# Cache compression as a ring of token-pair steps, with three split float32r products

## The chip, the core and the metric

The kernel runs on one core of a Trainium2 chip. The metric is device time in microseconds, the median of the runs. The core has five engines that run their own instruction lists and wait for each other by semaphores: TensorE (PE; its weight loads are shown as PEld), VectorE (DVE), ScalarE (ACT), GpSimd (POOL) and SyncE (SP). ACT, POOL and SP also issue DMAs.

## What is computed

One inference step of a decoder layer for a prompt of 1024 tokens and for 8 sequences that each have 8192 cached tokens and add one. The change is in the compression of the cache of the 8 sequences:

```python
r = CMP_BLOCK // CMP_STRIDE                      # 32 / 16 = 2
pieces = kv[:, :(n_c + r - 1) * CMP_STRIDE].reshape(b, n_c + r - 1, CMP_STRIDE, NSA_KV_HEADS, HEAD_DIM)
hid = sum(jnp.einsum('bncgd,cdf->bngf', pieces[:, p:p + n_c] + pe_r[p][:, None, :], w1_r[p]) for p in range(r))
return jnp.einsum('bngf,fd->bngd', jax.nn.gelu(hid), w2)
```

It is done for keys and for values (kv = 0, 1), for 8 sequences and 2 heads g of 64 channels. A sequence has 512 pieces of 16 tokens; a block is two pieces next to each other, so there are 511 blocks. The hidden width is 256. The cache lies in pages of 128 tokens, which a page table names. Beside it, the adaLN modulation is computed, c @ w_ada + b_ada, for 9 rows and 64 groups of 128 columns. All of it is float32.

## The kernel before

The kernel is a chain of stages with a barrier after each (`stage_done`); inside a stage the engines' lists are written by hand, each with its own semaphore waits.

The first stage, `setup`, loads the page table, turns two small tables, spreads the relative bias over 8193 distances on DVE (32 copies into `rev`), stores that table to HBM, and starts the loads of the compression weights, of the first modulation weights and of the first pages. Its store of 2 MB ends it.

The second, `cache_compress`, has 16 items, (i, kv), for 8 sequences i. An item's 64 pages go into `raw[:, kv]`, 32 by SP and 32 by POOL (`load_page`, line 168), once PE has turned what lay there. PE turns the pages, 16 tokens s of each piece, four 128 x 128 transposes each, into four banks (line 346). DVE copies the even tokens and ACT the odd ones into `xt` (line 412), so that a matmul contracts over two tokens of 64 channels. The first product (`first`, line 354) takes, for each of four quarters n = (g, c), a head and a half of the 256 hidden columns, 16 matmuls over 511 columns in fp32, each of which is two instructions in the profile. ACT applies the gelu (line 457), PE the second product (`second`, lines 366 and 369), DVE copies the result (line 423) and ACT stores it (lines 469 and 471). A quarter also has one of four pieces of the modulation (line 380, 16 instructions of 9 columns) and a quarter of the transposes of the item that follows. The position bias `peb` is a set of 128 one-column instructions ahead of it all (line 331).

Behind it come `load_x` (line 505 is its first DMA) and further stages. `mlstm_project` (line 649) is the third one after; its DVE list begins with two memsets and then waits for projections of the values (line 755). The last stages, merge, output and feed-forward, already use three split products: a float32 operand is rounded to float32r (ACT, line 2261), the rest is its difference (DVE, line 2285), and `mm3` (line 1909) sums high x high, high x low and low x high.

Of the kernel before, what the change touches and what calls it, by code (L numbers as in the profile page):

```python
# [34 lines left out]
B = 8  # L35
# [127 lines left out]
def load_page(k, eng, i, page, kv):  # L163
# [4 lines left out]
    eng.dma_start(k.raw[8 * q:8 * q + 8, kv, nt], pages[bass.ds(at, 1), :, :, P * kv:P * kv + P]  # L168
                  .rearrange("o n s c -> (o n) s c")).then_inc(k.s_page[kv][nt], 16)


def setup(k):

    nc = k.nc
    s_const, s_rows, s_vec, s_cT, s_cTs = (k.sem(x) for x in ("s_const", "s_rows", "s_vec", "s_cT", "s_cTs"))
    s_tab, s_rev, s_neg, s_fwd, s_store = k.sem("s_tab"), k.sem("s_rev"), k.sem("s_neg"), k.sem("s_fwd"), k.sem("s_bstore")
    with ExitStack() as ctx:
        crow = k.sb("crow", [9, D], ctx=ctx)  # L180
        vrow = k.sb("vrow", [NVEC, P], ctx=ctx)
        tab = k.sb("tab", [64, NBUCKET], ctx=ctx)
        rev = k.sb("rev", [64, NREV], ctx=ctx)
        fwd = k.sb("fwd", [H, NFWD], ctx=ctx)
        block = ctx.enter_context(nc.Block())
        ends = BUCKET_START[1:] + [PAST + 1]

        @block.sync
        def _(sp):
            sp.dma_start(k.pt[:, :], k.i["page_table"].rearrange("b n -> (b n)").rearrange("(o n) -> o n", o=1)).then_inc(k.s_pt, 16)  # L190
            sp.dma_start(crow[0:1, :], k.i["c_prompt"]).then_inc(s_rows, 16)
            sp.dma_start(crow[1:9, :], k.i["c_sample"]).then_inc(s_rows, 16)
            for name, (r, n) in VEC.items():
                a = k.i[name]
                a = a[0] if len(a.shape) == 2 else a
                sp.dma_start(vrow[r:r + n, :], a.rearrange("(r p) -> r p", p=P)).then_inc(s_vec, 16)
            sp.wait_ge(k.s_pt, 16)
            load_pages(k, sp, 0, 0, 0)

        @block.gpsimd  # L200
        def _(pool):
            pool.memset(k.ident[:, :], 0.0).then_inc(s_const, 1)
            pool.memset(k.ones[:, :], 1.0).then_inc(s_const, 1)
            pool.wait_ge(s_const, 2)
            pool.affine_select(out=k.ident[:, :], in_=k.ident[:, :], compare_op=ALU.not_equal, fill=1.0,
                               base=0, pattern=[[-1, P]], channel_multiplier=1).then_inc(s_const, 1)
            pool.wait_ge(k.s_pt, 16)
            load_pages(k, pool, 0, 0, 1)

        @block.tensor  # L210
        def _(pe):
            pe.wait_ge(s_const, 3)
            pe.wait_ge(s_rows, 32)
            for c in range(DK):
                mm = pe.transpose(k.bank[7][:, 9 * c:9 * c + 9], crow[:, P * c:P * c + P], k.ident[0:9, 0:9])
            mm.then_inc(s_cT, 1)
            pe.wait_ge(s_vec, 16 * len(VEC))
            pe.transpose(k.bank[6][:, 0:NVEC], vrow[:, :], k.ident[0:NVEC, 0:NVEC]).then_inc(s_cT, 1)

        @block.scalar  # L220
        def _(act):
            with nc.allow_non_contiguous_dma(reason="a 32 x 8 table, transposed"):
                for b in range(B):
                    act.dma_start(tab[8 * b:8 * b + 8, :], k.i["rel_bias"].rearrange("n h -> h n")).then_inc(s_tab, 16)
            load_cmp_weights(k, act, k.cw1, k.cw2, k.perow, (k.s_w1, k.s_w2, k.s_pe))
            for j in range(4):
                load_ada(k, act, 0, j)
            act.wait_ge(s_rev, NBUCKET)
            act.wait_ge(s_neg, 1)
            act.dma_start(k.biasrev_d, rev[:, :]).then_inc(s_store, 16)  # L230
            act.wait_ge(s_fwd, 3)
            act.dma_start(k.biasfwd_d, fwd[:, :]).then_inc(s_store, 16)
            act.wait_ge(s_store, 32)

        @block.vector
        def _(dve):
            dve.memset(rev[:, PAST + 1:NREV], NEG).then_inc(s_neg, 1)
            dve.wait_ge(s_cT, 1)
            dve.tensor_copy(k.cT[:, :, :], k.bank[7][:, 0:72].rearrange("p (c r) -> p c r", r=9)).then_inc(s_cTs, 1)
            dve.wait_ge(s_cT, 2)  # L240
            dve.tensor_copy(k.vecT[:, :], k.bank[6][:, 0:NVEC]).then_inc(s_cTs, 1)
            dve.wait_ge(s_tab, 16 * B)
            for n, (lo, hi) in enumerate(zip(BUCKET_START, ends)):
                dve.tensor_copy(rev[:, PAST - hi + 1:PAST - lo + 1],
                                tab[:, n:n + 1].to_broadcast([64, hi - lo])).then_inc(s_rev, 1)
            dve.wait_ge(s_rev, NBUCKET)
            dve.wait_ge(s_neg, 1)

            dve.tensor_copy(fwd[:, :], rev[0:H, PAST + 127:PAST + 127 - NFWD:-1]).then_inc(s_fwd, 1)
            dve.tensor_copy(k.bias_cmp[:, :], rev[:, 31:31 + 512 * STRIDE:STRIDE]).then_inc(s_fwd, 1)  # L250
            dve.tensor_copy(k.bias_win[:, :], rev[:, PAST - 511:PAST + 1]).then_inc(s_fwd, 1)


def load_pages(k, eng, i, kv, half):

    k.nc.disable_value_cache = True
    for page in range(NPAGES // 2 * half, NPAGES // 2 * (half + 1)):
        load_page(k, eng, i, page, kv)
    k.nc.disable_value_cache = False


def load_ada(k, act, m, j, final=False):

    w = k.i["w_ada_final"] if final else k.i["w_ada"][0]
    at = m * (4 * P) + (P * j - (48 * P if final else 0))
    act.dma_start(k.wada[:, j], w.rearrange("(k p) n -> p k n", p=P)[:, :, bass.ds(at, P)]).then_inc(k.s_ada[j], 16)
# [11 lines left out]
def cache_compress(k):  # L278

# [8 lines left out]
    s_page, s_w1, s_w2, s_pe = k.s_page, k.s_w1, k.s_w2, k.s_pe  # L288
    raw, w1, w2, perow = k.raw, k.cw1, k.cw2, k.perow
    s_peT, s_peTs, s_peb = k.sem("s_peT"), k.sem("s_peTs"), k.sem("s_peb")  # L290
    s_kst = [k.sem(f"s_kst{kv}", start=1) for kv in range(2)]
    s_tr, s_xtv, s_xta = k.sem("s_tr"), k.sem("s_xtv"), k.sem("s_xta")
    s_hid, s_gelu, s_kc, s_kcs = (k.sem(x, start=1) for x in ("s_hid", "s_gelu", "s_kc", "s_kcs"))
    s_zero, s_mod, s_modA = k.sem("s_hzero"), k.sem("s_mod"), k.sem("s_modA")
    s_modT = k.sem("s_modT", start=1)
    with ExitStack() as ctx:
        kc_vc = k.sb("kc_vc", [P, 2, NPIECE], ctx=ctx)
        peT = k.sb("peT", [P, 32], ctx=ctx)
        xt = k.sb("xt", [P, 2, G, 8, NPIECE], ctx=ctx)
        hid = k.sb("hid", [P, 2, 2, NPIECE], ctx=ctx)  # L300
        block = ctx.enter_context(nc.Block())

        def pages(eng, half):

            load_pages(k, eng, 0, 1, half)
            with eng.Fori(1, B) as i:
                for kv in range(2):
                    eng.wait_ge(s_tr, i * 32 + (16 * kv + 16 - 32))
                    load_pages(k, eng, i, kv, half)

        @block.sync
        def _(sp):
            pages(sp, 0)
            for kv in range(2):
                sp.wait_ge(s_kst[kv], 16 * B + 1)

        @block.gpsimd
        def _(pool):
            pages(pool, 1)

        @block.tensor
        def _(pe):
            pe.wait_ge(s_pe, 16)
            pe.transpose(k.bank[0][:, 0:32], perow[:, :], k.ident[0:32, 0:32]).then_inc(s_peT, 1)
            pe.wait_ge(s_peTs, 1)
            pe.wait_ge(s_w1, 32)
            pe.wait_ge(s_w2, 32)
            for kv in range(2):
                for c in range(2):
                    for j in range(16):  # L330
                        mm = pe.matmul(k.bank[1][:, 2 * kv + c:2 * kv + c + 1], w1[:, kv, j // 8, j % 8, P * c:P * c + P],
                                       peT[:, 16 * kv + j:16 * kv + j + 1], start=(j == 0), stop=(j == 15))
            mm.then_inc(s_peT, 1)
            pe.wait_ge(s_peb, 1)

            def turn(i, kv, tokens, start=False):

                for s in tokens:
                    if s == 0:
                        for nt in range(4):  # L340
                            pe.wait_ge(s_page[kv][nt], i * 256 + 256)
# [2139 lines left out]
```

## Time and profile before

| | us |
|---|---|
| runs: lowest, median, highest of 3 | 4170.76, 4171.27, 4180.03 |
| span of the profiled execution, first to last instruction | 4159.6 |
| what lies around the span, by the median | 11.7 |

| engine | busy us | share of the span |
|---|---|---|
| PE | 3572.3 | 86% |
| PEld | 2681.6 | 64% |
| DVE | 1200.2 | 29% |
| ACT | 721.6 | 17% |
| POOL | 459.6 | 11% |

How to read it: busy time is from the profile's records of instructions; a busy PE is not PE at its peak, since matmuls overlap and their ends are modelled. The distance between the starts of two matmuls, or the count of them in a stretch, is the better measure. Times in the timeline are from the first instruction. A "granted clock" of 1.00 is TensorE's 2.4 GHz, 0.50 is 1.2 GHz.

### The profile page before, as it was taken

The numbers are of one execution on the slowest core, as the hardware profiler recorded it, in microseconds if no ns is written. First come the engines' busy times: TensorE is split into PE (matmuls) and PEld (weight loads), VectorE is DVE, ScalarE is ACT, GpSimd is POOL, SyncE is SP. The second block draws the span as 40 slices with busy tenths as digits, with TensorE's granted clock in tenths as the row PEclk, the third lists the DMA queues.
The fourth block names the chain that finished last, engine by engine and source line by source line (L and its number), as shares of the span: only waits on it lengthen the run. The fifth ranks groups of instructions, "written<-read, shape, count | busy, mean of one in ns | idle before, by whom it ended". The sixth has DMA issues, their size and how long they took to land. (4 is left out here: it accounts for less than half of the span.)

```text
span 4159.6 us, 51003 instructions
## 1 busy us (share of the span) xinstructions
PE 3572.3 (86%) x16964; PEld 2681.6 (64%) x16964; DVE 1200.2 (29%) x2981; ACT 721.6 (17%) x1413; POOL 459.6 (11%) x692
## 2 busy tenths in 40 slices
PE   2899999999998796469699994578998779999997
PEld 1555555555555455355477772258887679999996
DVE  0111111111112104610155552112112344444445
ACT  0211111111111101200143340002111221111112
POOL 3222231322200000000000002720000000000000
PEclk9999999999999896669688876558999889999998
DMA  8455464545513100040300001313112212111111
GB/s 138 75 96 95 88 92 84 94 90 89 94 46 125 62 0 0 18 157 0 128 11 11 10 0 59 105 42 97 46 40 71 92 61 61 35 56 35 55 30 41
DMA packets 311388, 263.21 MB, mean 63 GB/s; under 512 B 45835, under 2 KB 282879, under 8 KB 310313
## 3 DMA queue, kind: packets, MB, share of 16 engines
q1 hardware_dynamic: 204184, 166.18, 15.5%
q0 software_dynamic: 31232, 50.90, 6.1%
q10 hardware_dynamic: 75792, 44.27, 5.1%
q14 instruction: 131, 1.07, 0.1%
q8 instruction: 49, 0.80, 0.1%
HBM read 232.71 MB, written 32.48 MB: 64 GB/s over the span
## 5 line engine op out<-in xcount | busy, mean ns | idle before, releaser
L354 PE MATMUL bank<-xt,cw 128*128 128x511 f32 x2048 | 892.4, 594 | 2.4 <-ACT xt L412 2.0
L354 PEld LDWEIGHTS bank<-xt,cw 128*128 128x128 f32 x2048 | 385.4, 191 | 469.4 <-issue 468.5
L412 DVE COPY xt<-bank 64x512 f32<-64x512 f32 x256 | 176.1, 688 | 937.5 <-PE bank L346 933.6
L168 POOL DMA_DIRECT2D raw<-in_cache_nsa_kv x512 | 310.3, 606 | 827.2 <-issue 827.2
L1909 PE MATMUL bank<-u2H,fwiH 128*128 128x344 f32 x1056 | 338.3, 320 | 38.2 <-DVE fwiL L2285 38.2
L1909 PE MATMUL bank<-u2H,fwiL 128*128 128x344 f32 x1056 | 337.9, 320 | 0.0
L1909 PE MATMUL bank<-u2L,fwiH 128*128 128x344 f32 x1056 | 337.8, 320 | 0.0
L1909 PEld LDWEIGHTS bank<-u2H,fwiH 128*128 128x128 f32 x1056 | 199.5, 189 | 38.7 <-issue 38.7
L1909 PEld LDWEIGHTS bank<-u2H,fwiL 128*128 128x128 f32 x1056 | 199.2, 189 | 0.0
L1909 PEld LDWEIGHTS bank<-u2L,fwiH 128*128 128x128 f32 x1056 | 198.9, 188 | 0.0
L412 ACT ACTIVATE xt<-bank 64x512 f32<-64x512 f32 x256 | 151.3, 591 | 160.4 <-PE bank L346 157.3
L457 ACT ACTIVATE hid<-bank,peb 128x511 f32<-128x511 f32 x64 | 44.0, 687 | 753.3 <-PE bank L354 753.3
L1909 PE MATMUL bank<-guH,gwgH 128*128 128x344 f32 x480 | 160.3, 334 | 15.1 <-DVE guT L2058 15.1
L1909 PE MATMUL bank<-fhH,fwoL 128*128 128x344 f32 x528 | 169.6, 321 | 0.0
L1909 PE MATMUL bank<-fhH,fwoH 128*128 128x344 f32 x528 | 168.7, 320 | 0.0
L1909 PE MATMUL bank<-fhL,fwoH 128*128 128x344 f32 x528 | 168.7, 320 | 0.0
L1900 DVE SCALAR_TENSOR_TENSOR xT<-bank,modT,xT 128x344 f32<-128x344 f32 (+1 forms) x264 | 148.6, 570 | 53.2 <-PE bank L1909 53.2
L1909 PE MATMUL bank<-guH,gwgL 128*128 128x344 f32 x480 | 153.7, 320 | 0.0
L1909 PE MATMUL bank<-guT,gwgH 128*128 128x344 f32 x480 | 153.5, 320 | 0.0
L1452 PE MATMUL bank<-kv,PTp 128*128 128x64 f32 x1056 | 149.1, 304 | 4.5 <-DVE oA L1549 4.5
L1452 PEld LDWEIGHTS bank<-kv,PTp 128*128 128x128 f32 x1056 | 147.8, 224 | 6.0 <-issue 4.9
L346 PE MATMUL bank<-ident,raw 128*128 128x128 f32 x1024 | 135.3, 289 | 13.7 <-issue 12.5
(436 smaller groups left out, 5063.1 us busy)
## 6 DMA issues: line engine op xcount, KB each, us to landing
raw<-in_cache_nsa_kv POOLq DMA_DIRECT2D x512, 64.0 KB, 4.8
raw<-in_cache_nsa_kv SPq DMA_DIRECT2D x512, 64.0 KB
wada<-in_w_ada ACTq DMA_DIRECT2D x48, 512.0 KB, 6.2
fwi<-in_w_ffn_in SPq DMA_DIRECT2D x44, 512.0 KB, 4.1
fwo<-in_w_ffn_out SPq DMA_DIRECT2D x22, 512.0 KB
gwg<-in_w_in SPq DMA_DIRECT2D x20, 512.0 KB, 3.9
wada<-in_w_ada_final ACTq DMA_DIRECT2D x16, 512.0 KB, 4.3
mw<-in_w_in SPq DMA_DIRECT2D x3, 2048.0 KB, 10.0
```

The costliest lines, as they stand in the source:

```text
L168: eng.dma_start(k.raw[8 * q:8 * q + 8, kv, nt], pages[bass.ds(at, 1), :, :, P * kv:P * kv + P] .rearrange("o n s c -> (o n) s c")).then_in ...
L346: mm = pe.transpose(k.bank[s % 4][:, P * nt:P * nt + P], raw[:, kv, nt, s, :], k.ident[:, :])
L354: mm = pe.matmul(k.bank[4 + c][:, 0:NCMP], w1[:, kv, j // 8, j % 8, P * c:P * c + P], xt[:, kv, g, j % 8, j // 8:j // 8 + NCMP], start=(j ...
L412: ins = eng.activation(dst, src, ACT.Copy) if odd else eng.tensor_copy(dst, src)
L457: act.activation(hid[:, g, c, 0:NCMP], k.bank[4 + c][:, 0:NCMP], ACT.Gelu_apprx_tanh, bias=k.peb[:, kv, c:c + 1]).then_inc(s_gelu, 1)
L1452: mm = pe.matmul(k.bank[7][:, HD * GATE[br]:HD * GATE[br] + HD], PT[0:tl[m][1], u % 2, t, :], v, start=(m == 0), stop=(m == len(tl) - 1))
L1900: dve.scalar_tensor_tensor(out=x, in0=bank[:, 0:w], scalar=k.modT[:, bass.ds(gate + c, 1), 0:1].rearrange("p o b -> p (o b)"), in1=x, op0= ...
L1909: mm = pe.matmul(out, a[x], b[y], start=start and n == 0, stop=stop and n == 2)
```

## The change

`setup` is gone as a stage; what it did is folded into `cache_compress`, and the bias tables are built in `mlstm_project`. The compression goes in 128 steps, 16 items of 8; step n is one pair of tokens of an item, and its matmuls are three split float32r products for both heads, both halves and both pieces of the block, summed over 8 steps in four banks. Pages are shared 24 (SP) to 40 (POOL), each queue with its own semaphores. The weights come in four chunks of 1 MB through the modulation's buffer and are split into `cwH` and `cwL`. The position bias is summed on DVE from multiply-adds and finished with four one-column matmuls. A whole modulation (four pieces) stands at the start of an item. In the lists below, `turn` turns one pair, the even token into bank 0 and the odd one into bank 1; `even` and `odd` copy these to `x32` (two copies of 64 x 512 each), `rounded` rounds them into slot n % 3 of `xH` and `rest` writes `xL = x32 - xH` (128 x 1024); `rest_w` does so for a chunk of weights (128 x 2048), and `pe_bias` is 8 multiply-adds of 128 x 256. The loops over items on PE, DVE and ACT are written out.

```diff
 PE
+            def turn(n):
+                i, kv, jj = n // 16, n // 8 % 2, n % 8
+                for odd in range(2):
+                    if n:
+                        pe.wait_ge(s_ca if odd else s_cd, n)
...
+                        mm = pe.transpose(k.bank[odd][:, P * nt:P * nt + P], raw[:, kv, nt, 2 * jj + odd, :], k.ident[:, :])
+                    mm.then_inc(s_tr, 1)
+            def first(n):
+                pe.wait_ge(s_xl, n + 1)
+                for g in range(G):
+                    for c in range(2):
+                        if jj == 0 and item:
+                            pe.wait_ge(s_gelu, 4 * item - 4 + 2 * g + c + 1)
+                        for r in range(2):
+                            w = slice(P * c, P * c + P)
+                            mm = mm3(pe, k.bank[2 + 2 * g + c][:, :], (wH[:, kv, r, jj, w], wL[:, kv, r, jj, w]),
+                                     (xH[:, n % 3, g, r:r + NPIECE], xL[:, n % 3, g, r:r + NPIECE]),
+                                     jj == 0 and r == 0, jj == 7 and r == 1)
+            turn(0)
+            turn(1)
...
+            for n in range(NSTEP):
...
+                if n == 5:
+                    modulation(0)
+                if item and n % 8 == 0:
+                    modulation(item)
+                if n + 2 < NSTEP:
+                    turn(n + 2)
...
+                first(n)
+                if item and n % 8 == 0:
...
+                    second(item - 1)
+            second(2 * B - 1)
 DVE
+            for m in range(2):
+                rest_w(m)
+                pe_bias(m)
+            for n in range(NSTEP):
+                even(n)
+                rest(n)
+                if n == 1:
+                    for m in range(2, 4):
+                        rest_w(m)
+                        pe_bias(m)
...
+                if n >= 8 and n % 8 == 2:
+                    shifted(n // 8)
+                    finish(n // 8 - 1)
 ACT
+            for n in range(NSTEP):
+                odd(n)
+                rounded(n)
+                if n == 0:
+                    round_w(2)
+                    round_w(3)
...
+                if n >= 8 and n % 8 == 1:
+                    gelu(n // 8 - 1)
+                if n % 8 == 3 and n > 8 or n == 7:
+                    m = (n + 1) // 8
+                    act.wait_ge(s_mod, m if n == 7 else m + 1)
...
+                            load_ada(k, act, m if n == 7 else m + 1, j)
+                if n >= 8 and n % 8 == 4:
+                    store(n // 8 - 1)
 SP (POOL has the same with SPLIT..NPAGES, SPLIT = 24)
+            load_pages(k, sp, 0, 0, 0, SPLIT, k.s_page)
+            load_pages(k, sp, 0, 1, 0, SPLIT, k.s_page)
+            with sp.Fori(1, B) as i:
+                for kv in range(2):
+                    sp.wait_ge(s_tr, i * 32 + (16 * kv - 16))
+                    load_pages(k, sp, i, kv, 0, SPLIT, k.s_page)
 mlstm_project
             sp.dma_start(gb[:, :], k.i["mlstm_gate_b"]).then_inc(s_gb, 16)
+            load_bias_table(k, sp)
             sp.wait_ge(s_fill, 4 * NG)
             sp.dma_start(w[:, 0], w_v[:, :, OFF_VB:OFF_VB + 512]).then_inc(s_w[0], 16)
+            store_bias_table(k, sp)
...
             sp.wait_ge(s_sm, 16)
+            sp.wait_ge(k.s_bst, 32)
...
         def _(dve):
+            spread_bias_table(k, dve)
             dve.memset(k.vb[:, :, :, MD:MD + 1], 1.0).then_inc(s_one, 1)
```

## Rows read from the trace of the kernel before

**Rows 1.** The page, part 1: busy us (share of the span) and instructions of each engine.
```profile
PE 3572.3 (86%) x16964; PEld 2681.6 (64%) x16964; DVE 1200.2 (29%) x2981; ACT 721.6 (17%) x1413; POOL 459.6 (11%) x692
```
**Rows 2.** The page, part 5: costliest groups; busy us, mean ns | idle ahead, releaser.
```profile
L354 PE MATMUL bank<-xt,cw 128*128 128x511 f32 x2048 | 892.4, 594 | 2.4 <-ACT xt L412 2.0
...
L412 DVE COPY xt<-bank 64x512 f32<-64x512 f32 x256 | 176.1, 688 | 937.5 <-PE bank L346 933.6
...
L412 ACT ACTIVATE xt<-bank 64x512 f32<-64x512 f32 x256 | 151.3, 591 | 160.4 <-PE bank L346 157.3
```
**Rows 3.** Timeline of PE, 120 to 300: start us, length us, line, tiles, count.
```profile
125.69 15.67 PE L354 MATMUL bank<-xt,cw 128*128 128x511 f32 x32 [1.97 <-ACT xt L412]
...
215.27 13.97 PE L354 MATMUL bank<-xt,cw 128*128 128x511 f32 x32
```
**Rows 4.** Timeline of PE, 640 to 790: pieces of an item.
```profile
654.87 13.97 PE L354 MATMUL bank<-xt,cw 128*128 128x511 f32 x32
...
703.06 1.85 PE L380 MATMUL bank<-cT,wada 128*128 128x9 f32 x16
704.76 1.99 PE L369 MATMUL bank<-cw,hid 128*128 128x64 f32 x16
706.57 3.58 PE L346 MATMUL bank<-ident,raw 128*128 128x128 f32 x16
...
744.67 1.95 PE L346 MATMUL bank<-ident,raw 128*128 128x128 f32 x16
746.45 13.87 PE L354 MATMUL bank<-xt,cw 128*128 128x511 f32 x32
760.16 1.85 PE L380 MATMUL bank<-cT,wada 128*128 128x9 f32 x16
```
**Rows 5.** Timeline of all engines, 1230 to 1345: the stage's last store, the next stage's first DMA.
```profile
1307.97 0.36 ACTq L471 DMA_DIRECT2D vc_d<-kc_vc  x1
...
1311.18 0.37 SPq L505 DMA_DIRECT2D xrow<-in_x_prompt  x1
```
**Rows 6.** Windows of PE, feed-forward: length, busy us (count), clock, DMA share, GB/s.
```profile
3500.00:3600.00 100.00, 100.00 (x638) 1.00 0.18 55
```
**Rows 7.** Windows of PE, compression: the same columns.
```profile
701.00:704.70 3.70, 3.70 (x22) 1.00 0.15 44
...
706.80:709.80 3.00, 3.00 (x16) 0.50 0.13 33
```
**Rows 8.** Timeline of all engines, 0 to 125.
```profile
5.53 118.77 SPq L168 DMA_DIRECT2D raw<-in_cache_nsa_kv  x51
...
8.96 6.40 DVE L244 COPY rev<-tab 64x1 f32<-64x1 f32 x32 [0.54 <-DMA tab<-in_rel_bias]
...
11.55 8.51 POOL L168 DMA_DIRECT2D raw<-in_cache_nsa_kv  x7 [0.64 <-issue]
...
84.64 27.47 PE L331 MATMUL bank<-peT,cw 128*128 128x1 f32 x128 [0.28 <-DVE peT L431]
```
**Rows 9.** Timeline of all engines, 3500 to 3506: a rounding and a subtraction, 1024 columns.
```profile
3504.19 1.05 ACT L2261 ACTIVATE fwiH<-fwi 128x1024 fp32r<-128x1024 f32 x1
...
3505.68 1.22 DVE L2285 TENSOR_TENSOR fwiL<-fwi,fwiH 128x1024 fp32r<-128x1024 f32 x1
```
**Rows 10.** The page, part 6: DMA issues, count, KB each, median us to landing.
```profile
raw<-in_cache_nsa_kv POOLq DMA_DIRECT2D x512, 64.0 KB, 4.8
...
wada<-in_w_ada ACTq DMA_DIRECT2D x48, 512.0 KB, 6.2
```
**Rows 11.** Timeline of SP's queue, 660 to 680.
```profile
660.75 19.64 SPq L168 DMA_DIRECT2D raw<-in_cache_nsa_kv  x10
```
**Rows 12.** Timeline of POOL, 600 to 760: the first and last of an item's 32 pages.
```profile
654.45 0.60 POOL L168 DMA_DIRECT2D raw<-in_cache_nsa_kv  x1 [28.49 <-issue]
...
697.06 0.60 POOL L168 DMA_DIRECT2D raw<-in_cache_nsa_kv  x1 [0.72 <-issue]
```
**Rows 13.** Timeline of DVE, 1370 to 1530: the stage the bias tables move to.
```profile
1501.04 0.69 DVE L755 COPY vb<-bank 128x512 f32<-128x512 f32 x1 [120.96 <-PE bank L711]
```

More of the change, by code:

```diff
@@ L168, in load_page @@
     eng.dma_start(k.raw[8 * q:8 * q + 8, kv, nt], pages[bass.ds(at, 1), :, :, P * kv:P * kv + P]
[L169 to L251, printed above, removed]
@@ L287, in cache_compress @@
     k.vc_d = k.dram("vc_d", (P, B, 4, P))
[L288 to L294, printed above, removed]
@@ L297, in cache_compress, with stage @@
         kc_vc = k.sb("kc_vc", [P, 2, NPIECE], ctx=ctx)
-        peT = k.sb("peT", [P, 32], ctx=ctx)
-        xt = k.sb("xt", [P, 2, G, 8, NPIECE], ctx=ctx)
-        hid = k.sb("hid", [P, 2, 2, NPIECE], ctx=ctx)
         block = ctx.enter_context(nc.Block())
[L303 to L309, printed above, removed]
+        def stage(m):
+            return k.wada[:, 2 * (m % 2):2 * (m % 2) + 2].rearrange("p a k n -> p (a k n)").rearrange("p (j f) -> p j f", f=CH)
@@ L325, in _ @@
[L325 to L341, printed above, removed]
-                    if not (start and s < 4):
-                        pe.wait_ge(s_xta if s % 2 else s_xtv, i * 16 + (8 * kv + s // 2 - 1))
-                    for nt in range(4):
-                        mm = pe.transpose(k.bank[s % 4][:, P * nt:P * nt + P], raw[:, kv, nt, s, :], k.ident[:, :])
-                    mm.then_inc(s_tr, 1)
@@ new lines, in modulation @@
+            def modulation(m):
+                pe.wait_ge(s_modT, m)
+                for j in range(4):
+                    pe.wait_ge(k.s_ada[j], m * 16 + 16)
+                    for c in range(DK):
+                        mm = pe.matmul(k.bank[6][:, 9 * j:9 * j + 9], k.wada[:, j, c, :], k.cT[:, c, :], start=(c == 0), stop=(c == DK - 1))
+                mm.then_inc(s_mod, 1)
+            pe.wait_ge(s_const, 3)
+            pe.wait_ge(s_pe, 16)
+            pe.transpose(k.bank[7][:, 0:32], perow[:, :], k.ident[0:32, 0:32]).then_inc(s_peT, 1)
@@ L434, in _ @@
[L434 to L441 removed]
+            dve.tensor_copy(peT[:, :], k.bank[7][:, 0:32]).then_inc(s_peTs, 1)
+            dve.wait_ge(s_cT, 1)
+            dve.tensor_copy(k.cT[:, :, :], k.bank[6][:, 0:72].rearrange("p (c r) -> p c r", r=9)).then_inc(s_cTs, 1)
@@ new lines, in round_w, with odd @@
+            def round_w(m):
+                kv, r = m // 2, m % 2
+                act.wait_ge(s_w1[r], kv * 16 + 16)
+                act.activation(wH[:, kv, r], stage(m), ACT.Copy).then_inc(s_wh, 1)
+            def odd(n):
+                act.wait_ge(s_tr, 2 * n + 2)
+                if n >= 2:
+                    act.wait_ge(s_xl, n - 1)
+                for g in range(G):
+                    ins = act.activation(x32[HD:P, n % 2, g, :], k.bank[1][HD * g:HD * g + HD, :], ACT.Copy)
+                ins.then_inc(s_ca, 1)
```

357 lines of the change are left out of this document (230 added, 127 removed).

## The prediction

> **What bounds the kernel now.** I read the page's busy shares first: PE has 86% of the span, no other engine over 29% [rows 1]. The costliest group is cache compression's first product, 2048 fp32 matmuls of 511 columns, 892.4 us busy with 2.4 us of idle ahead of them [rows 2]; the copies that feed it wait for PE, not the other way round. Then the timeline of PE inside that stage: from the first product of one item to that of the sixth after it (215.27 [rows 3] to 654.87 [rows 4]) are 439.6 us, 73.3 us an item. An item is four quarters, and the reader can add one up from starts: 32 matmuls from 746.45 to 760.16 are 13.71 us (428 ns each, two per fp32 product), 16 transposes from 744.67 to 746.45 are 1.78 us (111 ns each), 16 small matmuls of the modulation from 703.06 to 704.76 are 1.70 us, 16 of the second product from 704.76 to 706.57 are 1.81 us [rows 4]. 4 x (13.71 + 1.78 + 1.70) + 2 x 1.81 = 72.4 us. So the stage is PE, back to back; it starts its first product at 125.69 [rows 3] and the next stage's first DMA is issued at 1311.18 [rows 5]. That end, 1311.2 us, is what the change moves; everything after it stays as it was, except for the bias tables.
>
> **The product.** Before: 2048 x 0.428 = 877 us. After: 16 items x 8 steps x 24 float32r matmuls = 3072, of 512 columns. The trace has float32r only at 344 columns: 638 in 100 us, 156.7 ns each [rows 6], which is 13.4 ns over 344 columns at 2.4 GHz (143.3). fp32 at 511 columns takes two cycles a column (425.8) plus 2.6. So 512 columns cost 213.3 + 2.6 = 216 ns at least, 227 if the 13.4 is paid once per matmul, 233 if it grows with the columns (156.7 x 512/344). I take 227, since the trace's float32r row shows the 13.4; far end 429, if this operand (half of these matmuls start one column later) went at fp32's two cycles a column. 3072 x 0.227 = 697 us: 180 us less.
> The Trainium skill, "TensorE: Matmul & The Clock Gate", Back-to-back issue gap, gives N/2.4 + 2.5 ns, which is 216 ns here and a sum of 663 us. The row speaks against it for float32r: it would be 146 ns at 344 columns, and 157 is measured.
>
> **A step and an item after.** A step is 8 transposes (0.89) and 24 products (5.44): 6.33 us. Eight steps 50.6, the modulation, now in one piece, 4 x 1.70 = 6.8, second 3.6: 61.0 us an item on PE.
>
> **The clock.** Here a cost is added. The four modulation quarters, which lay between dense products, stand together: 6.8 us of nine-column matmuls, then 0.9 of transposes. The trace shows what this does: after 1.70 us of modulation and 1.81 us of the second product in a row, the 16 transposes at 706.57 took 3.58 instead of 1.95 us [rows 4], and the granted clock there is 0.50, the 1.2 GHz level, against 1.00 before [rows 7]. 128 one-column matmuls at the start went at 214 ns each (27.47/128) [rows 8], twice the modulation's 106. So behind such stretches the clock was found at the lower level, and work there takes twice as long. One such stretch cost 1.6 us; twice the length of small work makes me take two, 3.5 us an item. Bounds: 0, and 9 (all of the modulation and the transposes at half speed, and the first microsecond of the products). An item: 64.5 us.
>
> **The other engines in a step.** DVE: two copies of 0.688 [rows 2] and one subtraction over 1024 columns, 1.22 [rows 9]: 2.6. ACT: two copies of 0.591 [rows 2] and a rounding of 1.05 [rows 9]: 2.2, plus four gelus per item. Both lie under 6.3. The chain transposes, copy, rounding, subtraction, product is 0.4 + 1.4 + 1.05 + 1.2 and four hand-overs of some 0.25: about 5 us, and the transposes are issued two steps (12 us) ahead, so it is hidden; unhidden it would be 5 us a step. Added waits: before the transposes PE waits for both copies of the step before, queued behind it is the product of the step in hand; these copies end about 3 us into a 5.4 us product, so nothing. The gelus must free the four banks before step 0 of the next item; the modulation and the transposes (7.7 us) cover their four times 0.69. DVE's wait for the second product holds its next copy for one product, which the two steps of lead cover. The four modulation loads, each up to 6.2 us to landing [rows 10], are issued at step 3 for use five steps (32 us) later: hidden; were they not, 25 us an item.
>
> **Pages.** SP took 10 pages in 19.64 us [rows 11], 24 make about 48. POOL: 31 gaps between 654.45 and 697.06, 1.37 each [rows 12], 40 make 55. Both lie under the item's 64.5 (before: SP's 32 took 64 of 73). From the transposes that free a buffer to those that need it are nine products, eight groups of transposes, modulation and second, some 71 us, against 55 plus 4.8 to landing [rows 10].
> The Trainium skill, "SBUF — State Buffer", Who interferes with whom, says that a VectorE instruction with two SBUF inputs contends with a GpSimd one that reads SBUF, and that one in a two-port mode blocks it. The new subtraction has two SBUF inputs. The trace shows a hold of this kind for SBUF copies alone: while DVE spread the bias table (8.96 to 15.36), POOL's seven pages from 11.55 took 8.51 us, first to last end, with a hole after the first [rows 8].
> If each subtraction held POOL for its whole 1.22 us, eight an item, 55 becomes 65: just the item's length. I cost it at 0 and keep it as a rival.
>
> **The start.** Gone: setup's end, the 27.5 us of one-column matmuls [rows 8] and the long fill ahead of 125.69. What is late next is page 24 of SP: from 5.53, at 2.33 us a page (118.77/51) [rows 8], 61.5, landing 66. POOL's 40 at 1.37 land earlier, near 64. Then one pass of the chain, and two weight roundings (2 x 2.1) on ACT ahead of the second copy: first product at 74. Item 0: 50.6 of steps, 10 of modulation, about 7 in which DVE splits the second half of the weights (two subtractions of 2.4 and 16 multiply-adds of some 0.4, less one product that covers it), 2 for the clock's rise: item 1 starts at 144 (before 215.27).
> **The end.** 144 + 15 x 64.5 = 1111, last second product 3.6, copy 0.7, store 3.2 (1307.97 to 1311.18 [rows 5]), less 1.8 for the last item's missing transposes, and 4 for the stage's other small waits: 1121. Saved: 1311 - 1121 = 190 us.
>
> **Bias tables.** DVE in the stage they move to is idle 120.96 us ahead of 1501.04 [rows 13]; 32 spread copies and three more take some 8 us. SP's eight loads go ahead of a load that waits for half of the projection; the store of 2 MB follows that load and ends long before the stage. Cost 0; without that cover about 20 us.
>
> The span is 4159.6, the median of the runs 4171.3; I leave the 11.7 around the span as it is. 4171.3 - 190 = 3981.
>
> **Rivals.** (a) The clock holds: the four modulation pieces cost no more than now. For it: a single 1.70 us piece never lowered it. Against: [rows 7, 8]. 16 x 3.5 = 56 less: 3925. (b) The clock costs 9 an item: 16 x 5.5 = 88 more: 4069. (c) POOL becomes the bound: from 1.61 us a page (64.5/40) on. At 1.70, as when DVE holds it longer than its own 1.22, 68 us an item, 3.5 x 14 = 49 more: 4030. For it: the hole in [rows 8]; against: pages kept 1.37 beside DVE's copies. (d) The ring does not overlap as it is drawn: one hand-over a step shows, 1.4 us for 118 steps, 165: 4146. Against: two steps of lead. (e) Slower: float32r at 512 columns does not run one cycle a column. It decides from 227 + 190/3072 x 1000 = 289 ns on; at 429 it is 3072 x 0.202 = 621 more: 4602. For it only that the trace has no 512-column or odd-start row of it; against, 157 ns at 344, which is one cycle.
>
> **The numbers.** Forecast 0.48, (a) 0.20, (b) 0.06, (c) 0.15, (d) 0.06, (e) 0.05. The products' ends (216 and 233) move each by -34 and +18. The range 3915 to 4075 holds the forecast, (a), (b) and (c) with most of these and leaves out (d), (e) and the corner of (a) with 216. Within 0.3% (12 us, about what this kernel's runs can tell from no change) 0.01, faster 0.94, slower 0.05.
>
> **What would show it.** Right: float32r products near 227 ns with PE idle nowhere for long, an item of 64 to 65 us, first product near 74, next stage's DMA near 1121; the granted clock at 0.50 once an item, behind the modulation. Wrong: PE waiting for POOL's pages, products over 289 ns, or a step that is longer than its matmuls. What would overturn the whole is only (e).

## The result, and the profile after

The changed kernel takes 4000.95 us (median of 4 runs, 3991.6 to 4032.1) against 4174.35 for the kernel before, a ratio of 0.9595 [0.9558, 0.9633]: 173 us less. Predicted were 3981.0, which is 190 less, and 3915 to 4075 as the range. One run of the experiments (pages 32/32 with the modulation in one piece, 4330.9 us at a lower clock) was slow and is left out of its kernel's median. The profiled execution takes 3991.6 us, its span 3989.7.

The page's part 1, then its part 5 (busy us, mean ns of one | idle ahead, releaser), and its part 6 (median us to landing):

```profile
PE 3406.4 (85%) x17868; PEld 2874.1 (72%) x17868; DVE 1380.8 (35%) x3147; ACT 858.3 (22%) x1541; POOL 529.6 (13%) x820
...
L2013 PE MATMUL bank<-xH,cwH 128*128 128x512 f32 x1024 | 425.1, 415 | 0.0
...
L374 DVE COPY x<-bank 64x512 f32<-64x512 f32 x256 | 175.9, 687 | 417.8 <-PE bank L280 415.6
L472 ACT ACTIVATE x<-bank 64x512 f32<-64x512 f32 x256 | 151.4, 591 | 739.6 <-PE bank L280 612.4
L380 DVE TENSOR_TENSOR xL<-x,xH 128x1024 fp32r<-128x1024 f32 x128 | 157.0, 1227 | 240.0 <-ACT xH L481 240.0
...
wada<-in_w_ada ACTq DMA_DIRECT2D x48, 512.0 KB, 14.7
```
The one group of [rows 2] is now three of 1024 (L2013; a busy length counts overlap, so starts are read below), with no idle time ahead, and the copies still wait for PE: the stage is PE's as before. Its ends, from the timeline of PE at the start and of all engines at the end:

```profile
52.84 0.47 PE L280 MATMUL bank<-ident,raw 128*128 128x128 f32 x1 [36.26 <-DMA raw<-in_cache_nsa_kv]
59.98 1.88 PE L280 MATMUL bank<-ident,raw 128*128 128x128 f32 x7 [6.66 <-DMA raw<-in_cache_nsa_kv]
...
69.81 0.78 PE L2013 MATMUL bank<-xH,cwH 128*128 128x512 f32 x1
...
1148.19 0.33 ACTq L501 DMA_DIRECT2D vc_d<-kc_vc  x1
1151.36 0.39 SPq L604 DMA_DIRECT2D xrow<-in_x_prompt  x1
```
The first product starts at 69.8 instead of 125.7 [rows 3], the next stage's first DMA is issued at 1151.4 instead of 1311.2 [rows 5]: 159.8 us are won in the stage. The other 10 lie behind it: from that DMA to the end the span has 2838.3 us, before 2848.4. In the eleven kernels below, whose code there is the same, it has 2836 to 2849, so I count it to nothing.

An item seen from PE: at first two products of a step of the item before, 22 starts apart; then the modulation (the view starts inside it and shows 62 of its 64 matmuls), the transposes behind it, and products at the low clock:

```profile
897.45 0.40 PE L2013 MATMUL bank<-xL,cwH 128*128 128x512 f32 x1
...
902.61 0.40 PE L2013 MATMUL bank<-xH,cwL 128*128 128x512 f32 x1
...
941.76 9.24 PE L324 MATMUL bank<-cT,wada 128*128 128x9 f32 x62
950.86 1.95 PE L280 MATMUL bank<-ident,raw 128*128 128x128 f32 x8
952.45 0.78 PE L2013 MATMUL bank<-xH,cwH 128*128 128x512 f32 x1
953.03 0.63 PE L2013 MATMUL bank<-xL,cwH 128*128 128x512 f32 x1
...
956.01 0.63 PE L2013 MATMUL bank<-xH,cwL 128*128 128x512 f32 x1
```
Windows over the same place (length, busy us (count), granted clock, DMA share, GB/s):

```profile
946.30:956.50 10.20, 10.20 (x41) 0.50 0.39 80
956.50:1011.00 54.50, 54.45 (x280) 1.00 0.77 105
```
At the granted clock 1.00 (2.4 GHz) 22 products take 5.16 us, 234 ns each (233.1 over the stage); at 0.50 (1.2 GHz) seven take 2.98, 426 each. The modulation takes 9.2 instead of 6.8 us, because the clock falls inside it. Every item has such a stretch at 0.50, 6.8 to 13.7 us long; with the one behind a stop in item 14 the stage has 171 us at 0.50, that of the kernel before some 38. From the first product of item 1 (160.7) to that of item 15 (1091.9) are 931.2 us, 66.5 an item.

### The profile page after: what moved, and what is told of

It reads as the page before. It is cut to its first block and busy times, and to the rows that moved or that the text cites. A ratio compares the mean times of both kernels' runs of the same rounds, so it can differ in the third digit from the quotient of the medians.

```text
span 3989.7 us, 52799 instructions
## 1 busy us (share of the span) xinstructions
PE 3406.4 (85%) x17868; PEld 2874.1 (72%) x17868; DVE 1380.8 (35%) x3147; ACT 858.3 (22%) x1541; POOL 529.6 (13%) x820
## 5 line engine op out<-in xcount | busy, mean ns | idle before, releaser
L2013 PE MATMUL bank<-xH,cwH 128*128 128x512 f32 x1024 | 425.1, 415 | 0.0
L2013 PE MATMUL bank<-xL,cwH 128*128 128x512 f32 x1024 | 413.6, 404 | 0.0
L2013 PE MATMUL bank<-xH,cwL 128*128 128x512 f32 x1024 | 411.4, 402 | 0.0
L2013 PE MATMUL bank<-u2H,fwiH 128*128 128x344 f32 x1056 | 338.2, 320 | 38.4 <-DVE fwiL L2389 38.4
L2013 PE MATMUL bank<-u2H,fwiL 128*128 128x344 f32 x1056 | 337.8, 320 | 0.0
L2013 PE MATMUL bank<-u2L,fwiH 128*128 128x344 f32 x1056 | 337.6, 320 | 0.0
L374 DVE COPY x<-bank 64x512 f32<-64x512 f32 x256 | 175.9, 687 | 417.8 <-PE bank L280 415.6
L472 ACT ACTIVATE x<-bank 64x512 f32<-64x512 f32 x256 | 151.4, 591 | 739.6 <-PE bank L280 612.4
L380 DVE TENSOR_TENSOR xL<-x,xH 128x1024 fp32r<-128x1024 f32 x128 | 157.0, 1227 | 240.0 <-ACT xH L481 240.0
L2013 PEld LDWEIGHTS bank<-xH,cwL 128*128 128x128 f32 x1024 | 198.6, 194 | 47.2
L2013 PEld LDWEIGHTS bank<-xH,cwH 128*128 128x128 f32 x1024 | 200.9, 196 | 42.4
L2013 PEld LDWEIGHTS bank<-xL,cwH 128*128 128x128 f32 x1024 | 199.2, 195 | 41.4
L2013 PEld LDWEIGHTS bank<-u2H,fwiH 128*128 128x128 f32 x1056 | 199.4, 189 | 39.0 <-issue 39.0
L2013 PEld LDWEIGHTS bank<-u2H,fwiL 128*128 128x128 f32 x1056 | 199.1, 189 | 0.0
L2013 PEld LDWEIGHTS bank<-u2L,fwiH 128*128 128x128 f32 x1056 | 198.7, 188 | 0.0
L280 PEld LDWEIGHTS bank<-ident,raw 128*128 128x128 f32 x1024 | 134.5, 157 | 82.0 <-DMA raw<-in_cache_nsa_kv 43.7
L2013 PE MATMUL bank<-guH,gwgH 128*128 128x344 f32 x480 | 160.3, 334 | 14.9 <-DVE guT L2162 14.9
L2013 PE MATMUL bank<-fhH,fwoL 128*128 128x344 f32 x528 | 169.6, 321 | 0.0
L2013 PE MATMUL bank<-fhH,fwoH 128*128 128x344 f32 x528 | 168.7, 320 | 0.0
L2013 PE MATMUL bank<-fhL,fwoH 128*128 128x344 f32 x528 | 168.7, 320 | 0.0
## 6 DMA issues: line engine op xcount, KB each, us to landing
wada<-in_w_ada ACTq DMA_DIRECT2D x48, 512.0 KB, 14.7
```

The source lines that it names most:

```text
L280: mm = pe.transpose(k.bank[odd][:, P * nt:P * nt + P], raw[:, kv, nt, 2 * jj + odd, :], k.ident[:, :])
L374: ins = dve.tensor_copy(x32[0:HD, n % 2, g, :], k.bank[0][HD * g:HD * g + HD, :])
L380: dve.tensor_tensor(xL[:, n % 3, :, 0:NPIECE], x32[:, n % 2], xH[:, n % 3, :, 0:NPIECE], ALU.subtract).then_inc(s_xl, 1)
L472: ins = act.activation(x32[HD:P, n % 2, g, :], k.bank[1][HD * g:HD * g + HD, :], ACT.Copy)
L2013: mm = pe.matmul(out, a[x], b[y], start=start and n == 0, stop=stop and n == 2)
```

## The experiments

Times are medians of 3 runs or more. The end of the stage is the time of the next stage's first DMA in the profile. "Early" and "late" chunks are the second pair of the weight chunks, rounded before the steps begin or loaded during the first item.

**The modulation in pieces, as the kernel before had it.**
```diff
-                if item and n % 8 == 0:
-                    modulation(item)
+                if item and n % 2 == 0:
+                    piece(item, n % 8 // 2)
...
-                        for j in range(4):
-                            load_ada(k, act, m if n == 7 else m + 1, j)
+                    m, j = (n - 3) // 8, (n - 3) % 8 // 2
+                    act.wait_ge(s_mod, 4 * m + j + 1)
+                    load_ada(k, act, m + 1, j)
```


> The changed kernel with the modulation's 128 small matmuls cut into four pieces of 32, one behind every second step of the item, and its four loads issued one at a time. In the changed kernel each of the 16 items has 6.8 to 13.7 us at a granted clock of 0.50 behind the modulation, some 164 us of the stage in all, and I read half of it as lost. My theory: one block of 6.84 us of small matmuls is what lowers the clock, and pieces of about 1.7 us between products do not; the low stretches go (under 40 us are left in the stage), the items come to 61 to 62.5 us instead of 66.3, and with the stop at item 14 (6 us) the time falls by 60 to 80 us, to 3920 to 3940. Rival A: any stretch without products lowers the clock, so that four pieces lower it as long as one or longer: low time stays at 150 us or more, items 66 or more, 3990 to 4010 us. Rival B: the loss is not the clock's but the loads' that come in a burst: the next kernel, with the loads alone spread, then gains the same.


(It counts the small matmuls double: the rows show 64 an item, 16 a piece.) Measured 3916.2 us, ratio to before 0.9384 [0.9357, 0.9411]: 85 less than the changed kernel. Item 1 to item 15 are 860.6 us, 61.5 an item. A piece, the transposes behind it, and the stretch from item 1 to item 15 (length; busy us and count of PE, PEld, DVE, ACT and POOL; granted clock, DMA share, GB/s):

```profile
885.51 1.85 PE L324 MATMUL bank<-cT,wada 128*128 128x9 f32 x16
887.22 1.07 PE L280 MATMUL bank<-ident,raw 128*128 128x128 f32 x8
...
150.40:1011.00 860.60, 860.60 (x4764) 727.59 (x4761) 302.55 (x365) 288.42 (x392) 322.88 (x543) 1.00 0.73 107
```
and the same stretch of the changed kernel:

```profile
160.70:1091.90 931.20, 926.48 (x4762) 786.82 (x4761) 302.51 (x365) 288.43 (x392) 318.69 (x536) 0.93 0.65 98
```
The mean clock is 1.00 against 0.93, and the same instructions take 70.6 us less. That is what the low clock costs: 136 of the 931.2 us lie at 0.50, where products take 1.8 times as long and small matmuls up to twice, so 62 to 68 us are lost there, and TensorE is idle for 4.7. Rival A falls.

**The loads alone.**
```diff
+                if n >= 11 and n % 8 in (3, 4, 5, 6) and n // 8 + 1 < 2 * B:
+                    act.wait_ge(s_mod, n // 8 + 1)
+                    load_ada(k, act, n // 8 + 1, n % 8 - 3)
```


> The changed kernel with the modulation in one piece as it was, and only its four loads issued one to a step instead of four behind one another on ScalarE. My theory: ScalarE no longer stands 8 us in its issues, so item 14 loses its stop (4.06 us of TensorE's idle time and the low clock behind it, 72.5 against 66.3 us), and a load lands in 5 to 8 us instead of 14.7; the low stretches behind the modulation stay. 4 to 10 us faster than the changed kernel, 3990 to 3997. Rival B (the burst of loads is what the items lose): as much as with the modulation in pieces, 60 us or more. Rival C: nothing at all, since the loads are wanted only a whole item later.


Measured 4009.2 us, 0.9596 [0.958, 0.9612]: no gain, so rival B falls: the 85 us came with the pieces, and spread loads alone are worth nothing. The stretch from item 1 to item 15:

```profile
177.60:1108.80 931.20, 931.20 (x4762) 792.10 (x4761) 302.54 (x365) 288.87 (x392) 320.08 (x536) 0.92 0.60 98
```
It is as long as the changed kernel's. The stop in item 14 did go and a load landed in 8.0 us instead of 14.7, as expected, but the low stretches, 171 us in the changed kernel, are 181 here, so that nothing of it is left. What the stop was, from the changed kernel's timelines of ACT and PE:

```profile
1033.03 8.36 ACTq L184 DMA_DIRECT2D wada<-in_w_ada_final  x2
...
1042.72 9.24 ACTq L501 DMA_DIRECT2D vc_d<-kc_vc  x1
```
```profile
1053.31 1.11 PE L280 MATMUL bank<-ident,raw 128*128 128x128 f32 x4 [3.79 <-ACT x L472]
```
ScalarE stood in its DMA issues for 8.4 us (the last two of the four loads) and 9.2 us (a store), its copy was late, and TensorE waited 3.8 us; the item took 72.5.

**Pages 32/32, with the modulation in one piece.**
```diff
-    SPLIT = 24
+    SPLIT = 32
```


> The changed kernel with an item's 64 pages of tokens shared 32/32 between the two queues, as in the kernel before, instead of 24/40. From the rows of both kernels a page costs SP's queue 2.0 us and POOL 1.37 us: 32 pages are 65 us on SP, 44 on POOL. My theory: 65 us lies just inside an item of 66.3, so the share is worth 0 to 10 us in the steady state, plus what the first item's pages land later (they were 66 us for 24 on SP after the start, so up to 16 to 20 us more before the first product that needs the last of them). Together 10 to 25 us slower, 4010 to 4025. Rival A: SP binds outright, an item becomes 68 to 70 us: 16 items, 40 to 60 us slower. Rival B: no difference (under 4 us), the share is idle.


Measured 4022.4 us (4017.3 to 4044.9), 0.9653 [0.9611, 0.9695]: 21 more than the changed kernel, inside the 10 to 25 that I expected, and 13 more than the kernel with the loads spread. The intervals overlap with those of both, so a cost of this size is likely but not clear of the spread of the runs. In the profile the stage ends 30 us later, of which 20 are there at the first product (90.3 us, inside the 69.8 to 90.8 that kernels with 24 pages have) and 8 arise between item 1 and item 15. Of TensorE's waits between 150 and 1000 us (total, times, longest), this is the first:

```profile
PE bank L280 <- DMA raw<-in_cache_nsa_kv: 11.2, 4, 6.0
```
The changed kernel has none of these there. SP's 32 pages take 63.4 to 64.9 us, which fits an item of 66 us in most items only.

**Pages 32/32, with the clock held** (on the kernel with early chunks, below; the same edit).

> The kernel with the modulation in four pieces and the early chunks (3909.8 us, 61.5 us an item, no low clock in any item) with an item's pages shared 32/32 instead of 24/40. From the rows SP's 32 pages take 63.4 to 64.9 us in the changed kernel with that share. My theory: the share was worth little (4 stops, 14 us) only because the low clock had stretched the items to 66.3 us; at 61.5 SP binds, TensorE waits for pages in every item or every second, the items come to 64.5 to 66 us, and each stop lowers the clock behind it: 3960 to 4000 us. Rival A: the pages run ahead far enough, 10 to 20 us slower only, at most 3930 us. Rival B: the stops bring back the whole loss of the clock, items of 68 us and more, 4020 us or more.


Measured 4030.9 us, 0.9666 [0.9645, 0.9686], 121 more than its base. The same wait between 150 and 1000 us:

```profile
PE bank L280 <- DMA raw<-in_cache_nsa_kv: 61.4, 12, 10.2
```
105 us of the stage are at a low clock again (0.9 in the base), behind these stops; items take 67.9. My theory had the bound right and its price too low: rival B. So the share 24/40 is worth some 20 us as the change stands, not clear of the spread, and 121 once the items are short: 90 between item 1 and item 15, the rest mostly before item 1.

**One plain float32 product in the ring.**
```diff
-                            mm = mm3(pe, k.bank[2 + 2 * g + c][:, :], (wH[:, kv, r, jj, w], wL[:, kv, r, jj, w]),
-                                     (xH[:, n % 3, g, r:r + NPIECE], xL[:, n % 3, g, r:r + NPIECE]),
+                            mm = pe.matmul(k.bank[2 + 2 * g + c][:, :], wH[:, kv, r, jj, w], xH[:, n % 3, g, r:r + NPIECE],
```


> The changed kernel with the ring, the pairs, the folded setup and the shared pages as they are, but one plain float32 product in place of the three split float32r products (weights and tokens kept in float32; the split's remainders are still made by ScalarE and VectorE, and are not used). The kernel before took 0.857 us for such a product of 512 columns in its rows. A step is then 4 x 2 x 2 products of a quarter... by the rows: 64 products of the three become 64 of one, 16 a step; an item's products are 64 x 0.857 = 54.8 us as against 192 x 0.233 = 44.7 us. My theory: the three split products gave about 10 us an item and 160 us in all, nearly the whole gain, and the ring by itself gives little beyond the setup: 4150 to 4190 us. Rival A: the ring is what gave the gain (TensorE no longer waits for its copies), the products little: 4020 to 4080 us. Rival B: the clock matters as well: a plain float32 product keeps the clock up better or worse behind the modulation; to be read from the low time in the stage (164 us in the changed kernel, 34 us in the kernel before).


Measured 4169.7 us, 0.9993 [0.9979, 1.0007]: as before the change. Items take 76.8 us, 10.3 more than with split products; 64 x (0.858 - 3 x 0.233) is 10.2. Eleven records of such products, two of which make one product, and the stretch from item 1 to item 15:

```profile
879.63 4.89 PE L293 MATMUL bank<-xH,cwH 128*128 128x512 f32 x11
...
184.30:1259.40 1075.10, 1075.10 (x3867) 615.40 (x3866) 302.61 (x365) 289.62 (x392) 320.68 (x537) 0.93 0.56 85
```
Item 1's first product comes 31 us earlier than before (184.3 against 215.3 [rows 3]), and each item takes 3.5 longer than before's 73.3, 15 x 3.5 = 52, with 167 us at a low clock against some 38. So without the cheaper products the ring and the folded setup win 31 us at the start and lose them, and more, item by item: the gain is the products' (rival B on top, by the low time). Of the 178 us by which the stage ends later than in the changed kernel 21 are the start of this profile (first product 90.8 against 69.8), which differs from profile to profile; the rest are the items.

**One step of lead instead of two.**
```diff
-                if n + 2 < NSTEP:
-                    turn(n + 2)
+                if n + 1 < NSTEP:
+                    turn(n + 1)
```


> The changed kernel with a step's 8 transposes issued one step ahead of its products instead of two, all else as it is (modulation in one piece). Between a step's transposes and its first product stand the copy of VectorE or ScalarE (1.39 and 1.19 us), the rounding (1.06) and the subtraction (1.23): about 4 to 5 us with the handovers, against 5.6 us of products of the step in between at full clock. My theory (the ring hides its chain by far): one step of lead is nearly enough; only where the gelus stand between on ScalarE does TensorE wait, 1 to 3 us an item, and the kernel is 15 to 50 us slower than the changed kernel, 4015 to 4050 us. Rival A: the chain does not fit into a step, each of the 128 steps waits 1 us or more: 130 us slower or more, at or above 4130 us. Rival B: no change, then the second step of lead is idle.


Measured 4077.8 us, 0.9761 [0.9744, 0.9777]: 77 more, beyond my 15 to 50. One stop an item, at its first product:

```profile
892.65 0.76 PE L2012 MATMUL bank<-xH,cwH 128*128 128x512 f32 x1 [3.18 <-ACT hid L490]
```
It is the gelu that I named (12 stops, 39.4 us, between 150 and 1000 us; once TensorE also waits 9.3 us for the modulation's weights); for the subtraction, the end of the chain itself, products wait 2.0 us in all between 150 and 1000 us, so the chain fits a step. What I left out is the clock: behind these stops 276 us of the stage are low instead of 171, and an item is 71.5 us, 5.0 longer.

**Weight chunks 2 and 3 early, modulation in pieces.**
```diff
-            for m in range(2):
+            for m in range(4):
                 rest_w(m)
                 pe_bias(m)
```


> The kernel with the modulation in four pieces and its loads spread (3916 us), and beside that the second pair of weight chunks rounded, split and used for the position bias before the steps begin, in VectorE's idle 32 us at the start, instead of behind the first two steps. My theory: the 8.4 us for which TensorE waits on VectorE's copy behind that work go (82.5 to 90.9 in the profile of the kernel with the pieces), with the low clock behind the stop (10 us at 0.50, about 4 us lost): 8 to 13 us faster, 3903 to 3908. Rival A: the chunks land too late (they are issued at 23 to 30 us beside the pages), so that VectorE starts its first copy later by as much: no gain, 3910 to 3920. Rival B: what the start gives, the first item's pages take back, since the first product waits for the pages anyway.


Measured 3909.8 us, 0.9379 [0.9349, 0.941], with an interval that holds the ratio of the kernel with pieces alone (0.9384). In the profile item 0 takes 63.1 instead of 74.9 us and no item has a low stretch, as expected; the stage ends 10 us earlier. That is about the spread of the runs, so its worth in the time stays open.

**The same chunks late, pieces at even distances.**
```diff
+    AT = [10 + q * 117 // 63 for q in range(8 * B)]
...
+                if n in (1, 2):
+                    act.wait_ge(s_wl, n)
+                    act.wait_ge(s_acc, 8 * n)
+                    chunk(n + 1)
```


> The opposite of the kernel before in this list: the second pair of weight chunks (2 MB) is loaded, rounded, split and used only during the first item's steps, spread over steps 1 to 9, and the 64 modulation pieces stand at even distances over steps 10 to 127. The profiles differ in when the first product starts: 69.8 us in the changed kernel, 75.5, 86.9, 90.3 and 90.8 in the four kernels made from it, whose start is the same code; each time TensorE waits for the first item's pages on SP's queue, while the chunks are on their way. My theory: the 2 MB take the DMA engines from the pages, and without them the first product starts at 58 to 66 us in every run, so that this kernel gains the 8 us stop and 10 to 25 us of the start: 3885 to 3900 us, and its runs lie closer together. Rival A: the pages are slow by themselves (24 at 2.0 us on SP), the first product stays at 70 to 90: 3905 to 3915, as the kernel before. Rival B: the spread work makes ScalarE and VectorE late in the first item (3.3 us for each issue of a chunk), and what the start gives is lost in items 0 and 1.


Measured 3912.2 us, 0.9366 [0.935, 0.9381]. The start, with the chunks early (first fence) and late (second):

```profile
54.97 0.48 PE L280 MATMUL bank<-ident,raw 128*128 128x128 f32 x1 [38.46 <-DMA raw<-in_cache_nsa_kv]
68.60 1.76 PE L280 MATMUL bank<-ident,raw 128*128 128x128 f32 x7 [13.15 <-DMA raw<-in_cache_nsa_kv]
...
77.09 0.78 PE L2011 MATMUL bank<-xH,cwH 128*128 128x512 f32 x1
```
```profile
57.00 1.83 PE L281 MATMUL bank<-ident,raw 128*128 128x128 f32 x7 [15.78 <-DMA raw<-in_cache_nsa_kv]
...
65.57 0.78 PE L2017 MATMUL bank<-xH,cwH 128*128 128x512 f32 x1
```
My theory of the start holds: in the three profiles with late chunks the first product is at 65.1 to 65.6 us, in the seven that load them before the first product and have 24 pages on SP at 69.8 to 90.8 (the 90.3 in my expectation is the kernel with 32 pages). That the 2 MB take the DMA engines from the pages, as I wrote, is argued and not shown. What it gave was lost twice: item 1's pages, which do not come earlier, stopped TensorE for 10 us at 106, and four later items had 3.4 us at a clock of 0.50. These stood where a piece came directly behind the second product of values, 3.5 us of small matmuls ahead of the piece's 1.9; the four pieces directly behind the shorter second product of keys (1.9 us) had no low stretch:

```profile
199.78 2.29 PE L314 MATMUL bank<-cw,hid 128*128 128x64 f32 x19
201.91 1.91 PE L325 MATMUL bank<-cT,wada 128*128 128x9 f32 x16
203.66 1.34 PE L281 MATMUL bank<-ident,raw 128*128 128x128 f32 x8
...
204.30:207.70 3.40, 3.40 (x11) 0.50 0.65 69
```

**Late chunks, pieces away from the second product.**
```diff
-    AT = [10 + q * 117 // 63 for q in range(8 * B)]
+    AT = sorted([*range(10, NSTEP, 2), 21, 45, 69, 93, 117])
```


> The kernel with the late chunks (3912.2 us) with two things mended that its trace shows: five of its items had 3.4 us at a granted clock of 0.50 where an evenly spaced modulation piece stood directly behind the second product (1.94 to 3.68 us), and cost 3.4 us more than the others; here the pieces stand at every second step, away from the second product. VectorE's work on the late chunks is spread by one step more. My theory: all items from 1 on come to 60.7 and 62.2 us, the 10 us stop in item 0 for item 1's pages stays (these are bound by SP's first 48 pages, landing at 116 us), and item 1 starts at 130 to 133: 16 to 20 us faster than the kernel with the late chunks by the low stretches, 3892 to 3900 us, and 8 to 14 us faster than the one with the early chunks. Rival A: the low stretches were due to the pages' stop or other things: 3908 to 3915. Rival B: what is won at the start is lost by page waits in item 1 and 2.


Measured 3905.5 us, 0.9356 [0.9341, 0.9372]. The four low stretches (my expectation says five) are gone, which confirms where they came from; it gave 7 us, not 16 to 20, and the intervals of the two kernels overlap. Against early chunks nothing is won: both stages end at 1065.0, since item 1's pages stop TensorE for 9.2 us at 105 and the clock is low behind it (rival B, in item 1 itself).

**Halves in bfloat16** (first on the kernel with early chunks, then on the last one).
```diff
-        wH = k.sb("cwH", [P, 2, 2, 8, CH], F32R, ctx=ctx)
+        wH = k.sb("cwH", [P, 2, 2, 8, CH], BF16, ctx=ctx)
...
-        xH = k.sb("xH", [P, 3, G, XW], F32R, ctx=ctx)
+        xH = k.sb("xH", [P, 3, G, XW], BF16, ctx=ctx)
```


> The next kernel (modulation in four pieces, the second pair of weight chunks rounded before the steps) with the halves of weights and tokens kept in bfloat16 instead of float32r, three products as they are; this changes the precision of the compression. A float32r product of 512 columns follows the one before it after 233 ns in the changed kernel at a granted clock of 1.00, and one of 344 columns after 157: 0.4555 ns a column. Theory A: the operand's four bytes make the column cost more than one cycle (0.417 ns at 2.4 GHz): with two bytes a product follows after 213 to 217 ns, 3072 of them save 50 to 60 us, and items come to 58 instead of 61.5. Rival B: the column costs 0.4555 ns whatever the type: 233 ns again, and no more than 10 us saved, by shorter roundings. Rival C: the pages bind: POOL needs 55 us for an item's 40 and SP 48, both under 58, so that not yet.


Measured 3890.2 us, 0.9322 [0.9297, 0.9346], 20 less than its base. Products 22 starts apart:

```profile
882.50 0.38 PE L2012 MATMUL bank<-xL,cwH 128*128 128x512 bf16 x1
...
887.26 0.38 PE L2012 MATMUL bank<-xH,cwL 128*128 128x512 bf16 x1
```
4.76 us, 216.4 ns each: the price of theory A, 52 us of products; why four bytes cost more than two stays open. Only 27 of them reach the end of the stage (1037.6 against 1065.0), since rival C begins as well, with 20.5 us at 0.50 in those items:

```profile
PE bank L281 <- DMA raw<-in_cache_nsa_kv: 12.2, 4, 4.2
```


> The next kernel in this list (late chunks, modulation pieces never behind the second product) with the halves of weights and tokens in bfloat16, which changes the precision of the compression: products at 216 ns as measured (3072 x 17 ns = 52 us less than float32r), items 57.3 us of TensorE's work. The kernel with bfloat16 halves took 3890.2 us, with four waits for pages of 12.2 us in all and 23.7 us at a low clock. My theory: the start gains 6 to 10 us over it, and the page waits stay, since POOL's 40 pages need 53.4 to 54.5 us and land some 8 us after their issue, against 57.3 us for an item: 3875 to 3888 us. Rival A: the earlier start only turns into more page waits, since items 0 and 1 need 48 pages of SP by then: 3886 to 3895. Rival B: the pages are late in every item once the start no longer gives them a lead: 3900 or more.


Measured 3858.4 us, 0.9247 [0.9232, 0.9263], the fastest here, below my 3875 to 3888: the stage ends at 1011.9, and after the first stop (7.7 us at 102.5, for item 1's pages) TensorE has none of over 1 us. Why the other page waits of the first bfloat16 kernel are gone is not settled. Its precision in the compression is lower than the reference's float32; the fastest with the precision of the change is 3905.5.

## Why the prediction was right, and where it was off

- **PE sets the stage, the other engines and the chain are hidden.** Right. Between item 1 and item 15 PE is busy 926.5 of 931.2 us. Rival (d) falls: no hand-over shows in a step. One step of lead would hide the hand-overs too (2.0 us of waits); the second is worth its 77 us by the gelus and the clock behind their stops.
- **Product 227 ns.** It was the upper end, 233, paid by the column: 156.7/344 and 233.1/512 are both 0.455 to 0.456 ns a column. 3072 x 6 = 18 us missed. The Trainium skill, "TensorE: Matmul & The Clock Gate", Back-to-back issue gap, gives 216 ns, which it calls the isolated gap: the trace has that for the bfloat16 halves (216.4, in a stream) and not for float32r, at either width; the 131 ns that the section states for a stream at this width stand in no run here. Rival (e) falls.
- **The clock, 3.5 us an item.** The mechanism is shown (gathered small matmuls, not the loads), the size was too small: without the item that stopped, 66.05 - 61.47 = 4.6 us. I had the clock fall behind the block; it falls inside it. Rival (b), 9 us, falls. Rival (a) is what the change is with the modulation left in four pieces: 3925 was its forecast, 3916 the time.
- **Pages hidden.** Right: SP's 24 took 47.5 to 49 us, and from the first to the last of POOL's 40 are 39 gaps of 1.37 us, as in [rows 12]:

```profile
857.46 0.59 POOL L168 DMA_DIRECT2D raw<-in_cache_nsa_kv  x1 [10.88 <-issue]
...
910.71 0.59 POOL L168 DMA_DIRECT2D raw<-in_cache_nsa_kv  x1 [0.72 <-issue]
```

Rival (c) falls. The Trainium skill, "SBUF — State Buffer", Who interferes with whom, which I had read only for contention with GpSimd's reads, also says that `tensor_tensor`, the form of the subtraction, was not seen to stall DMA; the pages' spacing agrees.
- **Loads hidden.** Nearly: they landed in 14.7 us, not 6.2, since four go out together (8.0 where they are spread), TensorE waited 2.2 us for one in item 1, and once ScalarE's issue of them cost 6 us. I had priced their landing and not the time that the engine stands in issuing them.
- **The start.** First product 69.8 (predicted 74), item 1's modulation 146.9 (144), the stop for VectorE's split 8.3 (7). Right in this profile, partly by luck: the first product came 4 us early and item 0 up to that modulation took 77 us instead of 70, and over the profiles with this share the first product lies from 69.8 to 90.8, because I left out what the 2 MB of weight chunks do to the pages.
- **Bias tables 0.** Right. In the stage they moved to, VectorE's idle time is shorter by 16 us than in [rows 13], and from PE's first product there to the last store are 208.4 us in both kernels:

```profile
1337.95 0.69 DVE L859 COPY vb<-bank 128x512 f32<-128x512 f32 x1 [104.99 <-PE bank L814]
```
- **The sum.** Predicted end 1121, measured 1151.4. 28 of the 30 us are 14 items of 66.5 instead of 64.5: +1.15 product, +1.1 clock, +0.45 the stop in item 14, and -0.7, since an item with a full clock is 61.47 and not the 62.15 that my terms give at 233 ns (in the kernel with pieces its eight groups of transposes take 0.81 us each, not 0.89). The 10 us behind the stage, which I did not forecast and which lie within the spread of the profiles there, made up a third of it: that the total came so near is in part luck.

## What to carry to other kernels

Pieces of 1.7 us of small matmuls, each between dense products, cost only themselves here; gathered into one block they also lowered the clock for the products behind, so when a loop is rewritten, keep their places, and keep them away from other small matmuls. A stop of TensorE was paid twice in the same way (61.4 us of waits for pages came with 105 us at the low clock), so look at a queue that fits an item by 2 us only. Price a product by the column and by its type, from the width that the trace has.

## What the runs showed of the hardware that I had not expected

- The clock fell inside a block of 6.8 us of nine-column matmuls and stayed at 0.50 for 6.8 to 13.7 us, dense products included (426 ns each); four pieces of 1.7 us left it at 1.00 from item 1 on. A piece directly behind the 3.5 us of the values' second product was followed by 3.4 us at 0.50 in all four such items of one kernel, one behind the 1.9 us of the keys' in none of four.
- A float32r product of 512 columns follows after 233 ns, a bfloat16 one after 216.
- A DMA issue on ScalarE, a store's behind four loads of 512 KB, took 9.2 us, and its next copy waited; with the loads issued one to a step TensorE had no such stop left.
- With two more loads of 1 MB ahead of the first product it came 4 to 25 us later than in the three profiles without them, differently from profile to profile.
